# A two-block transformer kernel: work reordered around group ends, and half of the low weights made by GpSimd

## What is computed

```
# first layer
mod = silu(c) @ w_ada + b_ada;  shift, scale, gate = split(mod, 3)
h = rmsnorm(x, pre_g) * (1 + scale) + shift
q, k, v, gate_a, u, gate_p = split(h @ w_in)
y_a = windowed_attention(q, k, v, bias, sink) * silu(gate_a)      # 8 heads of 128
y_p = multiscale_pool(u, w_pool_grp, pool_scale) * silu(gate_p)
g_a, g_p = split(sigmoid(h @ w_merge + b_merge))
o = (g_a * (y_a @ w_br_attn) + g_p * (y_p @ w_br_pool)) @ w_out
x = x + gate * rmsnorm(o, post_g)
# second layer
mod = silu(c) @ w_mod + b_mod           # six parts
h = norm and modulate x
q_a, k_a, v_a, q_b, k_b, v_b, gk_lr, og_b, g_a, g_b = split(h @ w_in)
o_a = sliding_window_attention(rope(q_a), rope(k_a), v_a, sinks)  # 16 heads of 64, 4 kv heads
gk = log_sigmoid(gk_lr @ w_gk_up + b_gk) / 16
o_b = norm(gated_linear_attention(q_b, k_b, v_b, gk)) * silu(og_b)  # 4 heads, chunks of 64
x = x + g1 * rmsnorm((sigmoid(g_a)*(o_a @ w_br_a) + sigmoid(g_b)*(o_b @ w_br_b)) @ w_out)
u = causal_conv3(norm_modulate(x) @ w_up);  x = x + g2 * rmsnorm((silu(u1) * u2) @ w_down)
```

## Time and profile before

| | us |
|---|---|
| median of three runs | 2553.61 (2553.43 to 2560.65) |
| the profiled execution | 2549.6 |
| its span, first to last instruction | 2547.6 |
| TensorE busy, share | 2327.1, 91% |
| VectorE busy, share | 1752.9, 69% |
| ScalarE busy, share | 1096.2, 43% |
| GpSimd busy, share | 94.8, 4% |
| mean granted TensorE clock, share of full speed | 0.947 |

### The profile page before, as it was taken

The page is one execution under the profiler, slowest core; times in us unless marked ns, Lnnn a source line. Parts: engine busy times, 40 slices in busy tenths (PEclk is TensorE's granted clock), DMA queues, the critical chain, the costliest instruction groups (busy, mean ns, idle before and its releaser), DMA issues.

```text
span 2547.6 us, 31267 instructions
## 1 busy us (share of the span) xinstructions
PE 2327.1 (91%) x12900; PEld 1997.4 (78%) x12900; DVE 1752.9 (69%) x2043; ACT 1096.2 (43%) x1410; POOL 94.8 (4%) x113
## 2 busy tenths in 40 slices
PE   2499999999896878999999998897999999999998
PEld 1288888887785767778888887786888888888887
DVE  5867777778835776666677787745777777774443
ACT  1243354544445434444344443444444444444443
POOL 1000000000000000000011110000000000000000
PEclk7599999989997989999999999999999999999999
DMA  9967778878834746567877778843555555565553
GB/s 361 380 214 260 263 260 291 294 266 300 289 135 139 250 165 221 199 214 272 285 244 255 245 273 296 280 166 132 182 184 191 188 182 185 191 218 178 178 178 111
DMA packets 245121, 580.62 MB, mean 228 GB/s; under 512 B 11866, under 2 KB 14734, under 8 KB 240628
## 3 DMA queue, kind: packets, MB, share of 16 engines
q1 hardware_dynamic: 232320, 535.86, 60.5%
q0 software_dynamic: 11328, 40.26, 4.6%
q10 hardware_dynamic: 1332, 2.51, 0.3%
HBM read 557.61 MB, written 20.97 MB: 227 GB/s over the span
## 4 chain that ended last, share of the span: by engine, by line
PE 79%; DVE 11%; DMA 4%; ACT 3%; issue 2%; ACTq 0%; DVEq 0%; SPq 0%
PE gemm L1603 45%; PE gemm L1604 23%; DVE w_lo L977 3%; PE gemm L1607 3%; DMA lines<-line_rows 2%; DMA mod_stage<-in_w_mod 2%; DVE mod_acc L971 2%; PE extra L1407 2%; PE gemm L1606 1%; PE extra L1400 1%; ACT w_hi L645 1%; DVE quad_work L1020 1%; DVE operand_main L1024 1%; PE extra L1537 1%; ACT scores L645 1%
## 5 line engine op out<-in xcount | busy, mean ns | idle before, releaser
L1603 PE MATMUL gemm<-operand_main,w_hi 128*128 128x512 f32 x4567 | 1679.0, 408 | 101.7 <-DVE w_lo L977 29.3
L1604 PE MATMUL gemm<-operand_main,w_lo 128*128 128x256 f32 x4567 | 1299.9, 285 | 0.0
L977 DVE TENSOR_TENSOR w_lo<-w_stage,w_hi 128x1024 fp32r<-128x1024 f32 (+1 forms) x736 | 860.7, 1212 | 512.3 <-ACT w_hi L645 511.4
L1603 PEld LDWEIGHTS gemm<-operand_main,w_hi 128*128 128x128 f32 x4567 | 881.2, 193 | 314.3 <-issue 82.0
L645 ACT ACTIVATE w_hi<-w_stage 128x1024 fp32r<-128x1024 f32 (+1 forms) x736 | 731.9, 1044 | 845.3 <-PE gemm L1604 845.3
L1604 PEld LDWEIGHTS gemm<-operand_main,w_lo 128*128 128x128 f32 x4567 | 885.1, 194 | 13.9
L971 DVE SCALAR_TENSOR_TENSOR mod_acc<-mod_stage,c_silu,mod_acc 128x1024 f32<-128x1024 f32 x224 | 286.7, 1316 | 19.2 <-DMA mod_stage<-in_w_mod 13.4
L1603 PE MATMUL gemm<-ffn_hidden,w_hi 128*128 128x512 f32 x688 | 242.9, 397 | 0.0
L1604 PE MATMUL gemm<-ffn_hidden,w_lo 128*128 128x256 f32 x688 | 192.5, 280 | 0.0
L1603 PEld LDWEIGHTS gemm<-ffn_hidden,w_hi 128*128 128x128 f32 x688 | 129.1, 188 | 29.4
L1604 PEld LDWEIGHTS gemm<-ffn_hidden,w_lo 128*128 128x128 f32 x688 | 129.8, 189 | 0.8
(11 more groups left out here) (210 smaller groups left out, 1495.3 us busy)
## 6 DMA issues: line engine op xcount, KB each, us to landing
w_stage<-in_w_in SPq DMA_DIRECT2D x128, 1024.0 KB, 5.1
mod_stage<-in_w_mod SPq DMA_DIRECT2D x192, 512.0 KB, 6.0
w_stage<-in_w_up SPq DMA_DIRECT2D x88, 1024.0 KB, 5.0
w_stage<-in_w_down SPq DMA_DIRECT2D x44, 1024.0 KB, 5.1
w_stage<-in_w_ada SPq DMA_DIRECT2D x32, 1024.0 KB, 11.2
w_stage<-in_w_merge SPq DMA_DIRECT2D x32, 1024.0 KB, 5.4
w_stage<-in_w_out SPq DMA_DIRECT2D x32, 1024.0 KB, 5.1
mod_stage<-in_w_ada SPq DMA_DIRECT2D x32, 512.0 KB, 6.1
```

Source lines behind the costliest of these rows:

```text
L977: tt(WL[:, slot_of(n), c0:c1], WST[:, slot_of(n), c0:c1], WH[:, n % HIS, c0:c1].bitcast(F32), ALU.subtract)\
L1603: mm(G[:, m, :], hi, x_[:, k, :], start=(k == 0), stop=False)
L1604: ins = mm(G[:, m, T:2 * T], lo, x_[:, k, 0:T], start=False, stop=False)
```

## The change

- Each slab's second low half is made by GpSimd (`split_upper`), the first stays with VectorE; TensorE waits for both. GpSimd's other work in gates2 is placed by slab (`gates_of`).
- `mods_behind` puts rows only behind slabs that do not end a group, and the rows are dealt out anew: branch1 from 3 a phase to 1, out1 from 2, 2, 0, 0 to 3 each, qkvb from 5, 5, 4, 4 to 1, 3, 3, 3, og from 2 each to 2, 4, 4, 4, gates2 from 4 each to 4, 3, 3, 3, branch2 from 4 each to 3, 3, 1, 3, out2 from none to 4, 4, 4, 1.
- `mod_end` 4 and 8 stand behind resid, 5 to 7 move too.
- The gates' sigmoid is a hook of a branch phase's first slab. VectorE's wait for it stands behind the add that frees the bank.
- Half of the merged operand is made in the last branch phase into the attention operand (`merged_hi`), and out1 and out2 read from both.
- kv2 (keys and values) comes first, then gk, then q2. The rotation's tables are made during out1; its swapped rows are four ScalarE copies a set (`swap`) instead of permutation matmuls; rotation, z, softplus and scans are hooks. Attention reads q in place, its scale is folded into the add of the bias.
- gla6 and gla7 of a head run behind slabs 0 and 1 of the next gates2 phase, gla3 to gla5 behind slabs 4 to 6.

```diff
-        phases.append(Phase("u1", 0, [one(3072)], mod=(2, 0, 2)))
+        phases.append(Phase("u1", 0, [one(3072)], mod=(2, 0, 3)))
         for n, c in enumerate((0, 512, 1024, 1536)):
-            phases.append(Phase("in", n, [one(c)], mod=(2, 2 + 2 * n, 2),
-                                hooks={0: [("pool_sum", n)], 2: [("pool_mix", n)], 3: [("pool_out", n)]}))
+            phases.append(Phase("in", n, [one(c)], mod=(2, 3 + 2 * n, 2),
+                                hooks={0: [("pool_sum", n)], 1: [("pool_mix", n)], 2: [("pool_out", n)]}))
...
-            phases.append(Phase("in_gates", i, [one(2048 + 1536 * i)], mod=(2, 10 + 2 * i, 2)))
-        phases.append(Phase("gate_p1", 0, [one(4096)], mod=(2, 14, 2), post=[("mod_end", 2), ("silu1", 0), ("v1", 0)]))
+            phases.append(Phase("in_gates", i, [one(2048 + 1536 * i)], mod=((2, 11, 4), (2, 15, 1))[i],
+                                post=[("mod_end", 2)] if i else []))
+        phases.append(Phase("gate_p1", 0, [one(4096)], mod=(3, 0, 3), post=[("silu1", 0), ("v1", 0)]))
...
-                                hooks=attn(0, arg), late=[("attn5", arg)], mod=(3, 2 * i, 2), post=[("mod_end", 3)] if i == 7 else []))
+                                hooks=attn(0, arg), late=[("attn5", arg)], mod=(3, 3 + 2 * i, 2) if i < 5 else (3, 8 + i, 1),
+                                post=[("mod_end", 3)] if i == 7 else []))
...
-                                mod=(4, 3 * i, 3), pre=[] if i else [("poolmix", 0), ("prep_y", 1)]))
+                                hooks={0: [("gl_sig", i)], **({2: [("merged_hi", (0, 0)), ("merged_hi", (0, 1))]} if i == 3 else {})},
+                                mod=(4, i, 1), pre=[] if i else [("poolmix", 0), ("prep_y", 1)]))
...
-            phases.append(Phase("out1", i, [Group(A["w_out"][0], 512 * i, 4, "main", "proj", tile=16 + 4 * i)],
-                                hooks={2: [("out_sq", (0, i - 1))]} if i else {}, mod=(4, 12 + 2 * i, 2) if i < 2 else None,
-                                pre=[] if i else [("prep_merged", 0)], post=([], [("mod_end", 4)], [], [("resid", 0)])[i]))
+            phases.append(Phase("out1", i, [Group(A["w_out"][0], 512 * i, 4, "merged", "proj", tile=16 + 4 * i)],
+                                hooks=({1: [("rope_angle", 0)], 2: [("rope_angle", 1)]}, {0: [("rope_sin", 0)], 2: [("out_sq", (0, 0))]},
+                                       {2: [("out_sq", (0, 1))]}, {2: [("out_sq", (0, 2))]})[i], mod=(4, 4 + 3 * i, 3),
+                                pre=[] if i else [("prep_merged", 0)], post=[("resid", 0), ("mod_end", 4)] if i == 3 else []))
...
-        phases.append(Phase("gk", 0, [Group(w_in2, 5632, 4, "main", "proj", tiles=1, tile=59)],
-                            pre=[("prep_h", 1)], post=[("gla_gate", 0)]))
-        for i in range(3):
-            phases.append(Phase("qkv2", i, [two(512 * i, 4 * i)], mod=(5, 2 * i, 2), post=[("rope", 0)] if i == 2 else []))
+        phases.append(Phase("kv2", 0, [two(1024, 8)], pre=[("prep_h", 1)]))
+        phases.append(Phase("gk", 0, [Group(w_in2, 5632, 4, "main", "proj", tiles=1, tile=59)]))
+        phases.append(Phase("q2", 0, [two(0, 0)], hooks={0: [("v2", 0), ("swap", 0)], 1: [("z", 0), ("rope", 0)], 2: [("z", 1)]}, mod=(5, 0, 2)))
+        phases.append(Phase("q2", 1, [two(512, 4)], hooks={0: [("gk_abs", 0)], 1: [("swap", 1)], 2: [("rope", 1), ("gk_exp", 0)]}, mod=(5, 2, 2)))
...
+            behind = {**attn(0, pair[0]), **attn(4, pair[1])}
+            behind[4] = [("attn5", pair[0])] + behind[4]
+            if i == 0:
+                behind[1] = behind[1] + [("gk_ln", 0)]
+                behind[2] = behind[2] + [("gk_cum", 0)]
+                behind[4] = behind[4] + [("swap", 2)]
+                behind[5] = behind[5] + [("rope", 2)]
+                behind[6] = behind[6] + [("gk_cum", 1)]
             phases.append(Phase("qkvb", i, [two(1536 + 1024 * i, 12 + 8 * i), two(2048 + 1024 * i, 16 + 8 * i)],
-                                hooks={**attn(0, pair[0]), **attn(4, pair[1]), 3: [("attn4", pair[0]), ("attn5", pair[0])]},
-                                late=[("attn5", pair[1])],
-                                mod=((5, 6, 5), (5, 11, 5), (6, 0, 4), (6, 4, 4))[i], post=[("mod_end", 5)] if i == 1 else []))
+                                hooks=behind, late=[("attn5", pair[1])], mod=((5, 4, 1), (5, 5, 3), (5, 8, 3), (5, 11, 3))[i]))
...
-                                mod=(6, 8 + 2 * i, 2), post=[("mod_end", 6)] if i == 3 else []))
+                                mod=(6, 4 * i - 4, 4) if i else (5, 14, 2), post=[] if i else [("mod_end", 5)]))
...
-                                hooks={s: [(f"gla{s}", i)] for s in range(8)}, mod=(7, 4 * i, 4),
-                                post=[("mod_end", 7)] if i == 3 else []))
+                                hooks={0: ([("gla6", i - 1)] if i else []) + [("gla0", i)], 1: ([("gla7", i - 1)] if i else []) + [("gla1", i)],
...
+                                       2: [("gla2", i)], 4: [("gla3", i)], 5: [("gla4", i)], 6: [("gla5", i)]},
+                                late=[("gla6", 3), ("gla7", 3)] if i == 3 else [], mod=((6, 12, 4), (7, 0, 3), (7, 3, 3), (7, 6, 3))[i], post=[] if i else [("mod_end", 6)]))
...
-                                mod=(8, 4 * i, 4), pre=[] if i else [("prep_y", 2)]))
+                                hooks={0: [("gl_sig", 4 + i)], **({3: [("merged_hi", (1, 0))], 4: [("merged_hi", (1, 1))]} if i == 3 else {})},
+                                mod=((7, 9, 3), (7, 12, 3), (7, 15, 1), (8, 0, 3))[i], pre=[] if i else [("prep_y", 2)],
+                                post=[("mod_end", 7)] if i == 2 else []))
...
-            phases.append(Phase("out2", i, [Group(A["w_out_2"][0], 512 * i, 4, "main", "proj", tile=16 + 4 * i)],
+            phases.append(Phase("out2", i, [Group(A["w_out_2"][0], 512 * i, 4, "merged", "proj", tile=16 + 4 * i)],
                                 hooks={2: [("out_sq", (1, i - 1))]} if i else {},
-                                pre=[] if i else [("prep_merged", 1)], post=([("mod_end", 8)], [], [], [("resid", 1)])[i]))
+                                pre=[] if i else [("prep_merged", 1)], mod=((8, 3, 4), (8, 7, 4), (8, 11, 4), (8, 15, 1))[i], post=[("resid", 1), ("mod_end", 8)] if i == 3 else []))
...
-            behind = {5: [("ffn_sig", b)], 6: [("ffn_gate", b)]}
+            behind = {4: [("ffn_sig", b)], 5: [("ffn_gate", b)]}
...
-            return [r for r in range(rows) if r * len(ph.slabs) // rows == s]
+            free = [n for n, (g, q) in enumerate(ph.slabs) if q < g.slabs - 1]
+            return [r for r in range(rows) if free[r * len(free) // rows] == s]
...
+            def split_upper(n):
+
+                h, c0, c1 = halves(n)[1]
+                pool.wait_ge(hi_made, 2 * n + 2)
+                nc.gpsimd.tensor_tensor(WL[:, slot_of(n), c0:c1], WST[:, slot_of(n), c0:c1], WH[:, n % HIS, c0:c1].bitcast(F32),
+                                        ALU.subtract).then_inc(lo_made_pool, 1)
...
+            def gate_head(h):
+
+                pool.wait_ge(gs["og_in"], h * 16 + 16)
+                pool.wait_ge(gs["sig"], h + 1)
+                nc.gpsimd.tensor_tensor(OG[:, :, :], OG[:, :, :], VF[:, :, :], ALU.mult).then_inc(gs["gate"], 1)
...
+            def gates_of(i, s):
+
+                if s == 0:
+                    if i == 0:
+                        pool.wait_ge(gate_stored, 16 * 12)
+                        pool.wait_ge(biased, 16)
+                        pool.dma_start(CAUSAL[:, :], A["k_causal"]).then_inc(start["causal_in"], 16)
+                    else:
+                        gate_head(i - 1)
+                if s == 1:
+                    positive(pool, gs["y"], i * 4)
+                    pool.dma_start(OG[:, :, :], gates[1, 32 + 4 * i:36 + 4 * i].rearrange("t q n -> q t n")).then_inc(gs["og_in"], 16)
+                if s == 4:
+                    store_gate(1, first("gates2").groups[0] if i == 0 else named("gates2")[i].groups[0])
+                if s == 6:
+                    pool.wait_ge(gs["sq"], i + 1)
+                    nc.gpsimd.tensor_tensor(VF[:, 0:2, :], VF[:, 0:2, :], VF[:, 2:4, :], ALU.add).then_inc(gs["sq2"], 1)
+
...
+            for n in range(AHEAD):
+                split_upper(n)
...
+                for s in range(len(ph.slabs)):
+                    if ph.slab0 + s + AHEAD < len(slabs):
+                        split_upper(ph.slab0 + s + AHEAD)
+                    if ph.name == "gates2":
+                        gates_of(i, s)
...
+                if name == "gl_sig":
+                    act.wait_ge(gates_in, 32 * arg + 32)
+                    activate(GL[:, :, :, :], GL[:, :, :, :], ACT.Sigmoid).then_inc(sig_ready, 1)
+                if name == "merged_hi":
+                    blk, j = arg
+                    act.wait_ge(slab_used, merged_from[blk])
+                    act.wait_ge(merge_tiles, 8 * blk + 2 * j + 2)
```

(36 more changed lines are left out.)

322 lines of the change are left out of this document (153 added, 169 removed).

## The result

| | before | after |
|---|---|---|
| median, us | 2554.7 (2553.4 to 2560.7) | 2608.4 (2603.4 to 2612.9) |
| the profiled execution | 2549.6 | 2603.4 |
| ratio, 95% interval | | 1.0205 (1.0182 to 1.0229) |

The account below looks back on a forecast made before the run. TensorE, busy 91% of the span, bounds the kernel, so savings lie in its gaps and edges. Gains less charges sum to 65 us: 2549.6 to 2484.6, plus 4.0 for the median, 2489 us; range 2445 to 2558.

Parts of the forecast that it names:

- Rival A: GpSimd's operation falls where VectorE waits anyway; charges for gates2, up, in, merge and half the rows' fall away: 2460 us; chance 0.13.
- Rotation and decay gate: kv2, gk, q2: permutation matmuls leave TensorE and work between slabs rides behind q2 and qkvb slabs; gain 33 us.
- qkvb: Copies of q heads and y go, rows fall from 18 to 10, mod_end 5 moves out; gain 21 us.
- Up: Up stage: GpSimd's subtractions cost VectorE between 0 and 8 us over 88 slabs; 4 us taken.
- The operand and mod_end: Out phases: early half operand removes 4.05 us twice, mod_end behind resid saves some 4 each; out1 gains 10, out2 6.
- The waits of the branch phases: branch1, branch2: about 2.5 us of each stall stays in six of eight phases; branch1 gains 10, branch2 1.
- The lock: VectorE loses 2.07 to 2.65 us per collision with GpSimd's subtraction; charged up 4, merge and in phases 3.
- Rival C: VectorE operations that lost the lock delay group-end evacuations; half of 91 groups late by 2.3 us: 2595; chance 0.16.
- The rows: Four rows take 26 to 29 us against TensorE's 22.6; charged og 7, out2 4, in_gates 0 2 us.
- gates2 and branch2: gates2: idle at phase ends goes and returns elsewhere, gain 0, bounds +16 and -20; branch2 gains 1 us.
- B: New waits in the hand-ordered chains: gla2 late, four-row transfers serial, qkvb's idle only moved; 2525 us; chance 0.20.
- D: The change does not do what it says: stalls return at full size elsewhere, time stays 2550 us; chance 0.06.

Follow-up runs that it names:

- e1: The changed kernel with VectorE making both low halves of every slab again, the new order kept: 2537.7 us, ratio to before 0.9936.
- e4: The changed kernel with GpSimd's subtraction cut into four instructions of 256 columns: 2567.9 us, ratio to before 1.0052.
- e5: e1 with the modulation rows' transfers issued by GpSimd, one row ahead, instead of SyncE: 2574.1 us, ratio to before 1.0061.
- e7: e1 with the rows dealt out anew, at most three in a phase of four slabs, sums of parts 6 and 7 moved along: 2511.2 us.
- e14: e12 with GpSimd making every slab's second low half, its own two gates2 operations one slab earlier: 2550.1 us, ratio to before 0.9972.
- e9: e7 with the steps of linear attention behind the slabs of their own number again: 2491.3 us, ratio to before 0.9746.
- e12: e9 with the branch phases' gates transferred in two halves, the first a group earlier, and two half-size sigmoids: 2461.9 us, ratio to before 0.9629.
- e2: The kernel before with only GpSimd making each slab's second low half, its other gates2 operations placed by slab: 2676.9 us, ratio 1.0478.
- e10: e9 with GpSimd making the second low half in four quarters in branch1, qkvb, og and branch2 alone: 2497.4 us, ratio to before 0.9773.
- e11: The changed kernel with the attention denominators' two-tensor sum written as one tensor_scalar for each column: 2601.9 us, ratio to before 1.0178.
- e3: The changed kernel with GpSimd writing zeros three times over the second low half instead of subtracting: 2522.6 us, ratio to before 0.9873.

## Why the prediction was wrong

The difference of forecast and result is 119 us in the profiled executions. It splits at e1: GpSimd's share cost 67 (2603.4 less 2536.3), and I charged some 7 for it plus about 16 within gates2, so 44 are missed there; the order gained 13 where I had about 88 in the sum without those charges, 75 missed. (Rival A counts 6 us of the rows' charges to the lock as well; by that the split is 38 and 81.)

**The right steps.** Rotation and decay gate: 33 forecast, 31.4 in e1. qkvb: 21 forecast, 22.9. Up: +4 with bounds 0 and 8, +1.5. The operand and mod_end: the 4.05 us ahead of out1 are gone, mod_end 4 lies in the gap behind resid, out1's last slab with all that follows it keeps its length (30.4 before and 30.3 in e1), and the 4.42 us with its slow clock have left the middle of out1. The waits of the branch phases stay as read: 3.66, 3.51 and 3.72 in e1.

**The lock (44 us).** The mechanism was named and even priced too high: I took 2.07 to 2.65 us lost a slab, and 438 us over 368 operations are 1.2 (1739.1 less e1's 1747.1 plus 446). The failed step is the way from there to TensorE's time. For merge I added the loss to VectorE's load, got 5.5 to 6.1 of 6.2 us a slab and wrote 3 us; it cost 23.4. What is late there is not a load but a chain: bias, exponentials, sum, reciprocal, products, of which VectorE's queue holds most. In the kernel before TensorE never waits for it in merge; after, it waits in each of the eight phases, 23.4 us together, seven times 2.25 to 2.36, and the granted clock is 0.970 and not 0.992. In those seven phases VectorE loses the lock twice in the chain: 2.2 us at the low half ahead of it and 2.2 at the sum. Each time one low half of 1.22 us has been taken off, so some 2 us are left over, and the chain had no slack for them.

qkvb shows the other side. There the sum stands still as well, 2.35 us in each of its eight phases, but none of the 32 low halves does:

```profile
1056.81 1.21 DVE L1038 TENSOR_TENSOR w_lo<-w_stage,w_hi 128x1024 fp32r<-128x1024 f32 x1
...
1065.50 2.35 DVE L1253 TENSOR_TENSOR small<-small 128x4 f32<-128x4 f32 x1
...
1069.30 1.09 PE L1588 MATMUL extra<-identity,scores 128*128 128x128 f32 x8 [1.18 <-DVE scores L1260]
```

From the bias add to TensorE's start this chain takes 11.4 us, 10.3 in e1, and it begins as much earlier against TensorE. So the relief ahead of the chain makes the loss good, and in seven of the eight phases TensorE waits 1.1 to 1.3 us, as before (1.18 to 1.38) and as in e1. So the same lost lock costs 2.3 us or nothing, and VectorE's load does not tell which: the place in the chain does.

gates2 lost 19.4. Its waits for gla_k_end grow from 8.6 in e1 to 21.0 (6.0 to 7.1 us in three of the phases, in which the operation of that name stands for 2.56 us behind GpSimd's own product), and those for gla_k and gla_v by 3.9; which of the operations in these chains stand behind the subtractions was not taken apart, and e4 gave nothing back there.

Rival C had the sign and the cause, and mostly the wrong place. Evacuations read PSUM and kept their pace (conv_in 689 ns after, 688 before); the up stage, full of them, lost 1.5 us, though its low halves and gate products stood for up to 3.4 us. At group ends TensorE's waits for `proj` did grow, by 11.6 us against e1, those for merge_part and gate_out did not. By these waits I estimate that a sixth of the 67 us lies where C looked; it had half of the 91 groups late by 2.3 us each.

**The rows (38 us and more).** I found 26 to 29 us for four rows, and e5 shows 7.0 to 8.2 a row, so the size was right. I compared it with the 22.6 us of four slabs and let "the slabs in hand" take up the rest. The evacuation stands behind the rows, and the change itself packs them behind the first three slabs, two behind the first. What is late is due after three slabs, 17 us. So og, out2 and the first stretch paid 17.1, 12.2 and 12.2 where I had 7, -6 and 2: 38.5 of the 75. e7 takes 32 us back in these three stages (26.5 in the whole kernel, since gates2 and branch2 got the rows). out1 lost its gain in the same way (a wait of 5.28 us with three rows, 2.97 with two), branch1 and out1 together 11 us short of 20.

**gates2 and branch2.** My 16 us of recovered idle did not come in e1 either (+0.6 there, with no charge for the subtractions due): the waits for gate_out went, 11.9 us, and 8.6 for gla_k_end with 2.8 for gla_k came in their place. 7.6 of the 8.6 fall in the two phases in which VectorE's `gla_k_end` stands 2.2 us behind GpSimd's own product, which the new order has moved there; the prediction followed gla6 and gla7 on VectorE and not on GpSimd. Nor did it follow gla7's move past GpSimd's queue to the first gates, which cost branch2 7.6 us (11.23 against 3.66).

**Rivals.** B (new waits, 2525) comes nearest to e1, at 2538 somewhat worse. A is refuted by e1 and e14, D by the table: kv2 to q2, qkvb and branch1 kept most of what they gained.

What stays open: why merge is 5 us longer in e1 and e9 with e12 at 1.9, within what single executions differ; where in gates2 the subtractions cost 19.4 us; whether a second pair of buffers would free the rows; and the waits for the first evacuation of out1, out2 and kv2 to q2, 5.3, 6.5 and 6.8 us in e1, of which 2.8 to 6.8 are left in e9.

## What to carry to other kernels

Work given to GpSimd costs VectorE up to one whole GpSimd instruction for each operation that loses the lock. What this costs the kernel is read from the chains that end at TensorE, not from VectorE's load: count, for each chain, the operations that can lose the lock in it and ahead of it, take off the relief that stands ahead of it, and compare with its slack. That TensorE waits for nothing there today (merge) doesn't make a chain safe, and that it waits already (qkvb) doesn't make it dear. A busy share that doesn't fall when work leaves an engine is the sign. For a stream through one pair of buffers, multiply its round trip by the count and compare with the time at which the next thing behind it in the queue is due. When a step is moved, ask which queue's waits it takes along, and beside which operations of the other engine it comes to lie: e2 and e10 lost 23.5 and 6.3 us to one operation behind a wait for a later slab, and in e1 TensorE waited 2.7 us longer in each of the two phases of gates2 in which a product of GpSimd had come to lie beside VectorE's `gla_k_end` (3.79 against 1.07).

## What the runs showed of the hardware

Which of VectorE's operations stand still depends on what GpSimd does. Against its subtraction of two tensors: sums and products of two tensors in SBUF (the sum of two elements from 153 to 2054 ns), copies within SBUF (422 to 2448), tensor_scalars of 256 elements (0.61 to 2.16 us for two, e11). Against its memset (e3): copies (903) and tensor_scalars (811), and no two-tensor operation (154). Not hit by either, though GpSimd was at work beside them: operations with a PSUM operand (conv_in 692 ns in the 22 cases beside GpSimd's subtraction, 685 in the 22 others), the reciprocal (166 ns, e3 and e11), the maximum over 1024 elements (1220). A tensor_scalar of one element took 205 ns in all 48 cases beside the subtraction (e11); beside the memset no run has it. It is mutual: GpSimd's subtraction takes 2.5 us where it starts 1.0 us into VectorE's of 1.22, and 3.2 where it starts 0.3 us into it (185 and 11 cases in the kernel after).

The Trainium skill, "SBUF — State Buffer" (SBUF: two separate sides), says this lock is taken by an operation of VectorE "in a 2-port perf mode, or with two SBUF inputs (only against a GpSimd op that reads SBUF)". e3 and e11 agree with it in the forms listed above. The prediction had no row on copies and tensor_scalars; by the page they collide, and the runs bear it out. The sum would have been as wrong with that, for it missed where, not whether.

Transfers of 512 KB issued by GpSimd landed in a median of 5.3 us against 6.0 from SyncE's queue, and occupied GpSimd for 0.53 us each.
